# A two-block transformer on one core: sparse attention weighed in column halves, scaling shared by DVE and POOL, and waits and splits moved in three other stages

## Chip, cores and metric

The kernel runs on one core of a Trainium2 chip, as one program that is launched once. The metric is the device time of an execution in microseconds; a smaller time is better. Everything is computed in float32: PE takes a product either as f32 or as the sum of products of a high and a low part of its operands (type fp32r, names with hi and lo).

## What is computed

256 tokens of 1024 features pass through two blocks of two layers each.

```
first_block:   twice: h += 0.5 * swiglu(rmsnorm(h));  h += merged(conv, latent attention) @ w_o
                      h += 0.5 * swiglu(rmsnorm(h));  h += sigmoid(gate) * (p @ w_ple_proj);  then rmsnorm
second_block:  layer 0: h = gla_mixer(x)   (gated linear attention, chunks of 64)
               layer 1: h = nsa_mixer(x)   (sparse attention)
               each:    x = layer_norm(ALPHA * x + h);  x = layer_norm(ALPHA * x + moe_ffn(x))
nsa_mixer:     o = g0 * attention over 15 compressed blocks
                 + g1 * attention over selected blocks + g2 * attention over a window;  o @ w_out
```

With 256 tokens every block of 64 is selected and the window covers all, so the selected and the window branch are both causal attention over all keys, with keys and values of their own. There are 16 heads of 64 features in four groups that share keys and values. A head's two branches are each softmax(q k), times its gate, times v.

## The kernel before

All five engines run queues written out by hand, in program order, tied by semaphores; there is no scheduler. The weights come as a stream of units of 128 x 2048 values. For each unit SP loads halves into a ring of three raw slots (`fetch`), ACT copies them to a high part (`split_hi`, L773 and L775), DVE subtracts that for the low part (`split_lo`, L1160), and PE multiplies (`product`, L1945: high by high, high by low, low by high). A slot is free for ACT when PE has finished the unit three earlier. `units(n)` on ACT is n such splits; on DVE it is a split, and then the work on the results of a unit two earlier, which waits for PE. What else ACT and DVE have to do stands between the units, so its place in the queue sets when a unit gets ready. On PE, `take()` waits for the low part, and `settle(leave)` waits until all but `leave` of the pending banks of results have been read.

*Feed-forward* (`gate_up`, four times 11 trips of two units): a unit gives two blocks of 128 hidden features. For each block come eight products of high weights with both parts of x (512 columns, L2053) and eight of low weights with the high part (256 columns, L2056). The down projection (L2104, L2108) goes by up to sixteen and sixteen.

*Front of linear attention:* queries, keys, then values in four units, accumulated over all four in the four banks of psa, two banks per half of the tokens; then transposes and scores, the gate r, and states. ACT does logarithm and exponentials of the decay (L1041 to L1049) around DVE's scan (L1551 to L1558). DVE copies the values out, scaled, in two operations (L1573), with one signal after both.

*Front of sparse attention:* queries, compression of keys (two units) and of values (two units), keys, values. PE rotates the queries with a fixed matrix (L2533) into psd, once ACT has read the mixing gates there with a sigmoid (L1083); DVE finishes the rotation with two operations of 2048 elements (L1796, L1798), and POOL has made the product with the cosine before (L730).

*Sparse loop:* 32 items: i = t // 4 numbers a pair of heads, two items are its branches and two its sides (t % 2: the head within the pair). In trip t PE makes the scores of item t (mask L2261, L2628), turns the probabilities of item t - 2 (L2637) and weighs item t - 3 (L2654 to L2656: probabilities stationary, 64 columns of values moving). DVE takes the two row maxima (L1890, L1891) and copies every second turned item (L1897), ACT exponentiates (L1113, L1115) and copies the others (L1108). The probabilities are left unnormalised; per pair of heads DVE scales the 512 sums by gate over denominator (L1902, L1904, L1909), POOL adds the branches (L744), and PE turns the sum with two identity products onto the compressed branch (`nsa_gather`: L2665, L2669), from where ACT and DVE split it (L1121, L1887).

## Time and profile before

| | |
|---|---|
| Time, median of 3 runs | 1945.93 us (1942.67 to 1946.19) |
| The profiled execution | 1944.6 us, span of the trace 1942.8 us |
| Busy: PE, DVE, ACT, POOL | 1918.0, 1443.4, 1099.1, 36.6 us |
| Granted PE clock, mean over the span | 0.998 of 2.4 GHz |

The span is what the trace covers; the execution's time is 1.8 us longer. The profile gives each engine's busy time, the timeline of instructions with the idle time before each and what ended it, and the chain of waits that leads to the last instruction. A PE matmul's length in it includes its way through the array, so consecutive ones overlap, and the distance of their starts is what each costs. In the names, psa and psd are the two halves of PSUM, of four banks each, arena is the shared work space in SBUF, w_hi and w_lo the parts of a unit of weights, x_both and y_both both parts of an operand.

### The profile page before, as it was taken

How to read it: one execution, taken by the hardware profiler on the slowest of the kernel's cores; microseconds unless marked ns; L12 is line 12 of the kernel's file. 1: busy time of each engine (PE TensorE's matmuls, PEld its weight loads, DVE VectorE, ACT ScalarE, POOL GpSimd, SP SyncE). 2: the span in 40 equal slices, each digit the busy share in tenths (PEclk: the TensorE clock that was granted, in tenths of full speed). 3: DMA queues.
4: the chain of work that ended last, by engine and by line, in shares of the span. 5: the costliest groups of instructions: out<-in, count | busy, mean ns of one | idle time of the engine just before them, and what ended most of it. 6: DMA issues, size and time to landing. Idle time of an engine off the chain costs nothing.

```text
span 1942.8 us, 30918 instructions
## 1 busy us (share of the span) xinstructions
PE 1918.0 (99%) x12146; PEld 1714.2 (88%) x12146; DVE 1443.4 (74%) x1867; ACT 1099.1 (57%) x1453; POOL 36.6 (2%) x37
## 2 busy tenths in 40 slices
PE   9999999999999999999999999999999999999998
PEld 7888999998889888999998889888888898997887
DVE  6775777777757776686678766775799887568997
ACT  6654545565547654555556545544677663656775
POOL 0000000000000000000000000000000010001000
PEclk9999999999999999999999999999999999999999
DMA  7656555355555566555355665442799744038994
GB/s 284 194 191 194 189 196 174 125 178 189 192 194 178 190 193 194 194 191 172 118 184 191 194 192 192 144 155 66 288 359 380 293 152 152 1 109 309 368 374 161
DMA packets 89683, 388.33 MB, mean 200 GB/s; under 512 B 10096, under 2 KB 10096, under 8 KB 74832
## 3 DMA queue, kind: packets, MB, share of 16 engines
q1 hardware_dynamic: 88992, 383.87, 57.7%
q0 software_dynamic: 560, 2.60, 0.3%
q8 instruction: 96, 1.57, 0.3%
q14 instruction: 35, 0.29, 0.0%
HBM read 385.38 MB, written 1.05 MB: 199 GB/s over the span
## 4 chain that ended last, share of the span: by engine, by line
PE 92%; DVE 4%; ACT 1%; DMA 1%; DVEq 1%; issue 1%; SPq 0%; POOL 0%; ACTq 0%
PE psa L1945 38%; PE psd L2053 9%; PE psa L2053 8%; PE psd L1945 7%; PE psd L2056 4%; PE psa L2104 4%; PE psd L2104 4%; PE psa L2056 4%; PE psd L2108 2%; PE psa L2108 2%; PE psa L2628 1%; PE psa L2275 1%; DVE w_lo L1160 1%; DMA raw<-weights 1%; PE psd L2637 1%
## 5 line engine op out<-in xcount | busy, mean ns | idle before, releaser
L1160 DVE TENSOR_TENSOR w_lo<-raw,w_hi 128x1024 fp32r<-128x1024 f32 x496 | 588.4, 1228 | 194.5 <-ACT w_hi L773 191.5
L773 ACT ACTIVATE w_hi<-raw 128x1024 fp32r<-128x1024 f32 x250 | 263.4, 1054 | 296.7 <-PE psa L1945 171.2
L1945 PE MATMUL psa<-x_both,w_hi 128*128 128x256 f32 x1984 | 360.7, 284 | 1.2 <-DVE arena L1573 0.7
L1945 PEld LDWEIGHTS psa<-x_both,w_hi 128*128 128x128 f32 x1984 | 309.7, 192 | 2.8 <-DVE arena L1573 0.9
L1945 PE MATMUL psa<-x_both,w_lo 128*128 128x256 f32 x992 | 280.6, 283 | 0.0
L775 ACT ACTIVATE w_hi<-raw 128x1024 fp32r<-128x1024 f32 x250 | 261.4, 1046 | 4.9 <-DMA raw<-weights 4.9
L1945 PE MATMUL psa<-w_hi,slots_x 128*128 128x512 f32 x640 | 201.8, 396 | 0.7 <-DVE w_lo L1155 0.5
L1945 PEld LDWEIGHTS psa<-x_both,w_lo 128*128 128x128 f32 x992 | 190.3, 192 | 0.0
L1155 DVE TENSOR_TENSOR w_lo<-raw,w_hi 128x2048 fp32r<-128x2048 f32 x60 | 138.9, 2315 | 12.3 <-ACT w_hi L768 11.3
L1945 PEld LDWEIGHTS psa<-w_hi,slots_x 128*128 128x128 f32 x640 | 116.6, 188 | 25.6 <-DVE w_lo L1155 2.5
L1945 PE MATMUL psa<-w_lo,slots_x 128*128 128x512 f32 x320 | 125.2, 391 | 0.0
L768 ACT ACTIVATE w_hi<-raw 128x2048 fp32r<-128x2048 f32 x60 | 114.9, 1915 | 9.8 <-PE psd L1945 9.8
L1945 PE MATMUL psa<-y_both,w_hi 128*128 128x256 f32 x608 | 110.4, 284 | 1.8 <-issue 1.8
L2053 PE MATMUL psd<-x_both,w_hi 128*128 128x512 f32 x384 | 98.8, 394 | 0.6 <-DVE x_both L1179 0.6
L1945 PE MATMUL psd<-w_hi,x_both 128*128 128x512 f32 x320 | 99.0, 390 | 0.0
L2053 PE MATMUL psd<-y_both,w_hi 128*128 128x512 f32 x384 | 98.6, 393 | 0.0
L1945 PEld LDWEIGHTS psa<-y_both,w_hi 128*128 128x128 f32 x608 | 94.9, 192 | 2.2 <-ACT arena L1016 2.1
L1155 DVE TENSOR_TENSOR w_lo<-raw_y,w_hi 128x2048 fp32r<-128x2048 f32 x36 | 85.5, 2374 | 13.4 <-ACT w_hi L768 13.4
L2104 PE MATMUL psa<-hid_both,w_hi 128*128 128x512 f32 x352 | 86.6, 391 | 0.0
L2104 PE MATMUL psd<-hid_both,w_hi 128*128 128x512 f32 x352 | 86.6, 391 | 0.0
L1945 PE MATMUL psa<-y_both,w_lo 128*128 128x256 f32 x304 | 86.0, 283 | 0.0
L2053 PE MATMUL psa<-x_both,w_hi 128*128 128x512 f32 x320 | 80.2, 392 | 1.0 <-DVE act_gate L1193 1.0
(423 smaller groups left out, 3487.2 us busy)
## 6 DMA issues: line engine op xcount, KB each, us to landing
raw<-weights SPq DMA_DIRECT2D x500, 512.0 KB, 4.8
raw<-weights SPq DMA_DIRECT2D x60, 1024.0 KB, 6.8
raw_y<-weights SPq DMA_DIRECT2D x36, 1024.0 KB, 6.8
x<-weights SPq DMA_DIRECT2D x18, 1024.0 KB, 6.4
h<-x_in SPq DMA_DIRECT2D x1, 1024.0 KB, 5.0
result<-h SPq DMA_DIRECT2D x2, 512.0 KB, 2.8
sml<-smalls POOLq DMA_DIRECT2D x1, 831.0 KB, 10.3
cst<-consts POOLq DMA_DIRECT2D x1, 683.5 KB, 7.7
```

Of the source, the lines that this page charges most:

```text
L768: act.activation(w_hi[:, s, :], raws[r], ACT.Copy).then_inc(hi_done, 2)
L773: act.activation(w_hi[:, s, UNIT_HALVES[0]], raw[:, s, UNIT_HALVES[0]], ACT.Copy).then_inc(hi_done, 1)
L775: act.activation(w_hi[:, s, UNIT_HALVES[1]], raw[:, s, UNIT_HALVES[1]], ACT.Copy).then_inc(hi_done, 1)
L1155: dve.tensor_tensor(w_lo[:, s, :], raws[r], w_hi[:, s, :], ALU.subtract).then_inc(lo_done, 2)
L1160: dve.tensor_tensor(w_lo[:, s, c], raw[:, s, c], w_hi[:, s, c], ALU.subtract).then_inc(lo_done, 1)
L1945: ins = pe.matmul(out, lhs, rhs, start=first and n == 0, stop=last and n == 2, skip_group_check=True)
L2053: pe.matmul(out, hi, operand[2][:, :, k, :], start=k == 0, stop=False, skip_group_check=True)
L2056: ins = pe.matmul(out[:, 0:T], lo, operand[0][:, k, :], start=False, stop=k == KD - 1, skip_group_check=True)
L2104: pe.matmul(out, parts(s, at * P, at * P + P)[0], hid_both[:, k], start=k == 0, stop=False, skip_group_check=True)
L2108: ins = pe.matmul(out[:, 0:T], parts(s, at * P, at * P + P)[1], hid_both[:, k, 0, :], start=False, stop=k == HB - 1, skip_group_check=True)
L2275: ins = pe.matmul(out[:, P * tt:P * tt + keys], a, b, start=False, stop=tt == 1 and n == len(terms) - 1, skip_group_check=True)
L2628: ins = pe.matmul(out[:, P * tt:P * tt + keys], nsa_q[:, i, tt * P:tt * P + P], (nsa_ks, nsa_kw)[branch][:, i // 4, side_of, 0:keys], star ...
```

## The change

**Sparse loop.** Scores use four banks of psa rather than three, and probabilities four buffers each before and after turning. The denominators are kept per item, and DVE makes for each item, one trip after its maxima, a reciprocal, a product with the gate and the scaling of the first 128 columns; POOL scales the other 256; only then may PE turn the item (three trips after its scores). PE weighs two items, both sides, at every second trip: the values are stationary now, 64 columns each, and the two sides write partitions 0 to 63 and 64 to 127 of a bank of psd, on which the compressed branch was put first. The scaled sums, their addition by POOL and the identity products are gone. The last projection waits for the last two pieces of its operand, where it waited for one.

**Feed-forward.** A unit does the high products of both blocks and then the low ones of both; first_half is signalled behind the first block's low products.

**Front of linear attention.** PE waits for the last bank before the values only where it writes that bank; DVE signals the values of the first half of the tokens on their own, and PE goes on when their two banks are free. ACT splits one unit more before the three exponentials, one less behind.

**Front of sparse attention.** ACT's sigmoid comes one unit earlier. On DVE the first hidden-row copy and two units' splits come before the two 2048-wide operations of the rotation.

```diff
@@ gpsimd
-            for i in range(KD):
-                pool.wait_ge(parts_ready, i + 1)
...
+            for t in range(2 * NHEADS):
+                pool.wait_ge(share_ready, t + 1)
+                part = nsa_probs[:, t % 4, P:384]
+                pool.tensor_scalar(part, part, nsa_share[:, t % 4, 1:2], None, ALU.mult).then_inc(p_ready, 1)
@@ scalar, linear attention
             act.activation(gla_t, gla_t, ACT.Ln, bias=1.0).then_inc(act_out, 1)
-            units(1)
+            units(2)
...
             act.activation(gla_kend, gla_t, ACT.Exp, scale=1.0 / GTAU).then_inc(act_out, 1)
-            units(4)
+            units(3)
@@ scalar, sparse front
-            units(3)
+            units(2)
             act.wait_ge(pe_to_act, seen.more(pe_to_act))
             act.activation(nsa_gates, psd[:, 0, 0:96].rearrange("p (a c) -> p a c", a=2),
                            ACT.Sigmoid).then_inc(mix_known, 1)
-            units(1 + 2 + 1)
+            units(1 + 1 + 2 + 1)
@@ scalar, sparse loop
-            for t in range(items + 7):
-                if 0 <= t - 2 < items:
+            for t in range(items + 5):
+                if 0 <= t - 3 < items:
...
-                if t >= 10 and (t - 10) % 4 == 0:
-                    i = (t - 10) // 4
+                if t >= 8 and t % 4 == 0:
+                    i = (t - 8) // 4
                     act.wait_ge(o_summed, seen.more(o_summed))
-                    act.activation(y_hi[:, i, :], psa[:, 3, 0:T], ACT.Copy).then_inc(xh_ready, 1)
+                    act.activation(y_hi[:, i, :], psd[:, 2 + i % 2, 0:T], ACT.Copy).then_inc(xh_ready, 1)
@@ vector, linear attention, values_scaled
                                             psa[:, 2 * tt:2 * tt + 2, :], rms_by_token[:, tt:tt + 1], None, ALU.mult)
+                    if tt == 0:
+                        ins.then_inc(evac, 1)
@@ vector, sparse front
             mark(for_pe)
             units(1, None)
+
+            def hidden_rows(kind, bank):
+                return lambda _: dve.tensor_copy(nsa_hid_rows[0:CROWS, kind, :], psa[0:CROWS, bank, 0:CHID])
+            units(1, hidden_rows(0, 3))
+            units(1, None)
             dve.wait_ge(pe_out, seen.more(pe_out))
             dve.wait_ge(queries_by_cos, 1)
...
-            units(1, hidden_rows(0, 3))
-            units(1, None)
@@ vector, sparse loop
+                if 0 <= t - 1 < items:
+                    u = t - 1
+                    i, branch, side_of = u // 4, u % 4 // 2, u % 2
+                    dve.wait_ge(exp_done, seen.more(exp_done))
+                    step(dve.reciprocal(nsa_share[:, u % 4], nsa_den[:, u % 4]))
+                    step(dve.tensor_tensor(nsa_share[:, u % 4], nsa_share[:, u % 4], g_c[:, :, 2 * i + side_of, 1 + branch],
+                                           ALU.mult))
+                    part = nsa_probs[:, u % 4, 0:P]
+                    dve.tensor_scalar(part, part, nsa_share[:, u % 4, 0:1], None, ALU.mult).then_inc(share_ready, 1)
+                if 0 <= t - 3 < items:
                     turn_of_t = seen.more(t_done)
-                    if t % 2 == 1:
+                    if (t - 3) % 2 == 1:
                         dve.wait_ge(t_done, turn_of_t)
-                        dve.tensor_copy(nsa_probs_t[1], psd[:, 1, 0:384]).then_inc(odd_pt_ready, 1)
...
+                        dve.tensor_copy(nsa_probs_t[:, (t - 3) % 4], psd[:, 1, 0:384]).then_inc(odd_pt_ready, 1)
@@ tensor, gate_up
-                    else:
-                        ins = block(0, range(KD))
-                        if part == 1:
-                            ins.then_inc(first_half, 1)
-                        ins = block(1, range(KD))
+                        for j in range(2):
+                            high(j, ks)
+                        for j in range(2):
+                            ins = low(j, ks)
+                            if part == 1 and j == 0:
+                                ins.then_inc(first_half, 1)
@@ tensor, linear attention
-            settle()
+            settle(1)
             for m in range(4):
...
                         for half in range(2):
+                            if tt == 1 and half == 1:
+
+                                settle()
...
-            pending.append(evac)
+            pending += [evac, evac]
...
-            settle()
+            settle(1)
...
+            settle(2)
             dense(2, KD, 2, x, signal=r_scaled, bank=2)
@@ tensor, sparse loop
             def nsa_weigh(t):
...
+                i, branch = t // 4, t % 4 // 2
+                out = psd[:, 2 + i % 2, 0:T]
+                if branch == 0:
...
+                    pe.matmul(out, nsa_vc[:, i // 4, i % 2, :], nsa_pt[:, i // 2, :], start=True, stop=False,
+                              skip_group_check=True)
+                pe.wait_ge(odd_pt_ready, seen.more(odd_pt_ready))
+                for k in range(TT):
+                    for side_of in range(2):
+                        keys = nsa_probs_t[:, (t + side_of) % 4, (0, T)[k]:(T, 384)[k]]
+                        ins = pe.matmul(out[DH * side_of:DH * side_of + DH, P * k:T],
+                                        nsa_v[:, branch, k, 2 * (i // 4) + side_of, :], keys, start=False,
+                                        stop=branch == 1 and k == 1, skip_group_check=True)
...
+            for t in range(items + 4):
                 if t < items:
                     nsa_score(t)
-                if 0 <= t - 2 < items:
-                    nsa_turn(t - 2)
+                if t >= 5 and t % 2 == 1:
+
+                    pe.wait_ge(pt_ready, seen.more(pt_ready))
                 if 0 <= t - 3 < items:
-                    nsa_weigh(t - 3)
+                    nsa_turn(t - 3)
...
+                if t >= 5 and t % 2 == 1:
+                    nsa_weigh(t - 5)
-            out_projection((KD - 1,), o_done, late_residual=True)
+            out_projection((KD - 2, KD - 1), o_done, late_residual=True)
```

Three places show how the instructions stand. On PE in the middle of the sparse loop, one item before:

```order
L2261 MATMUL psa<-mask_bf,ident_bf 128x2x128
L2628 MATMUL psa<-arena 128x128
L2628 MATMUL psa<-arena 128x256
L2637 MATMUL psd<-cst,arena 128x128 [waits exp_done]
L2637 MATMUL psd<-cst,arena 128x128 x2
L2654 MATMUL psd<-arena 128x64 [waits odd_pt_ready]
L2655 MATMUL psd<-arena 128x64
L2656 MATMUL psd<-arena 128x64
```

and in the change, the second trip of a pair:

```order
L2250 MATMUL psa<-mask_bf,ident_bf 128x2x128
L2621 MATMUL psa<-arena 128x128
L2621 MATMUL psa<-arena 128x256
L2630 MATMUL psd<-cst,arena 128x128 [waits p_ready,pt_ready]
L2630 MATMUL psd<-cst,arena 128x128 x2
L2643 MATMUL psd<-arena 128x256 [waits o_done]
L2649 MATMUL psd<-arena 64x256 [waits odd_pt_ready]
L2649 MATMUL psd<-arena 64x256
L2649 MATMUL psd<-arena 64x128 x2
```

The turns now wait for POOL's p_ready in place of ACT's exp_done, the trip before has no weighing, and the compressed product (L2643, every second time) stands here and not in a gather of its own.

On DVE in the sparse loop, a trip with a copy, before and in the change:

```order
L1890 TENSOR_REDUCE arena<-psa 128x1 [waits s_done]
L1891 TENSOR_REDUCE arena<-psa 128x1
L1897 COPY arena<-psd 128x384 [waits t_done]
```

```order
L1886 TENSOR_REDUCE arena<-psa 128x1 [waits s_done]
L1887 TENSOR_REDUCE arena<-psa 128x1
L1893 RECIPROCAL arena<-arena 128x2 [waits exp_done]
L1894 TENSOR_TENSOR arena<-arena 128x2 [waits dve_step]
L1897 TENSOR_SCALAR arena<-arena 128x128 [waits dve_step]
L1902 COPY arena<-psd 128x384 [waits t_done]
```

The copy, for which PE's weighing waits, stands three operations further from the scores.

On DVE in the front of sparse attention, before and in the change (the operations of 2048 elements are the rotation, those of 62x256 the hidden rows):

```order
L1160 TENSOR_TENSOR w_lo<-raw,w_hi 128x1024 [waits hi_done] x2
L1796 TENSOR_TENSOR arena<-psd,cst 128x2048 [waits queries_by_cos,pe_out]
L1798 TENSOR_TENSOR arena<-arena,x 128x2048 [waits dve_step]
L1160 TENSOR_TENSOR w_lo<-raw,w_hi 128x1024 [waits dve_step,hi_done]
L1160 TENSOR_TENSOR w_lo<-raw,w_hi 128x1024 [waits hi_done]
L1802 COPY arena<-psa 62x256 [waits unit_done]
L1160 TENSOR_TENSOR w_lo<-raw,w_hi 128x1024 [waits hi_done] x2
L1806 TENSOR_SCALAR arena<-arena 128x96 [waits mix_known]
```

```order
L1154 TENSOR_TENSOR w_lo<-raw,w_hi 128x1024 [waits hi_done] x4
L1792 COPY arena<-psa 62x256 [waits unit_done]
L1154 TENSOR_TENSOR w_lo<-raw,w_hi 128x1024 [waits hi_done] x2
L1797 TENSOR_TENSOR arena<-psd,cst 128x2048 [waits queries_by_cos,pe_out]
L1799 TENSOR_TENSOR arena<-arena,x 128x2048 [waits dve_step]
L1802 TENSOR_SCALAR arena<-arena 128x96 [waits dve_step,mix_known]
```

Two units are subtracted (four halves) in one go, and the rotation stands behind the first hidden rows and a third unit.

## Rows read from the trace of the kernel before

**Rows 1.** The page, part 1: busy us, share of span, instructions by engine
```profile
PE 1918.0 (99%) x12146; PEld 1714.2 (88%) x12146; DVE 1443.4 (74%) x1867; ACT 1099.1 (57%) x1453; POOL 36.6 (2%) x37
```

**Rows 2.** Timeline, PE, feed-forward: start us, length us, engine, line, operation, tiles
```profile
60.64 2.00 PE L2053 MATMUL psd<-x_both,w_hi 128*128 128x512 f32 x8
...
66.22 2.00 PE L2053 MATMUL psd<-x_both,w_hi 128*128 128x512 f32 x8
...
138.85 3.82 PE L2104 MATMUL psa<-hid_both,w_hi 128*128 128x512 f32 x16
...
144.42 1.55 PE L2104 MATMUL psa<-hid_both,w_hi 128*128 128x512 f32 x6
```

**Rows 3.** Timeline, PE, front of linear attention; [idle us before <-releaser]
```profile
1257.15 0.71 PE L1945 MATMUL psa<-w_hi,x_both 128*128 128x512 f32 x2 [0.99 <-DVE arena L1193]
...
1270.27 0.74 PE L1945 MATMUL psa<-w_hi,x_both 128*128 128x512 f32 x2 [1.97 <-DVE w_lo L1160]
...
1284.83 0.50 PE L1945 MATMUL psa<-x_both,w_hi 128*128 128x256 f32 x2 [0.68 <-DVE arena L1573]
...
1291.27 2.86 PE L2461 MATMUL psd<-arena 128*128 128x256 f32 x12 [0.44 <-DVEq L1141]
```

**Rows 4.** Timeline, ACT and DVE, the same front
```profile
1263.92 1.06 ACT L1047 ACTIVATE arena<-arena 128x1024 f32<-128x1024 f32 x1 [6.66 <-DVE arena L1558]
...
1267.85 2.36 DVE L1160 TENSOR_TENSOR w_lo<-raw,w_hi 128x1024 fp32r<-128x1024 f32 x2 [3.97 <-ACT w_hi L773]
...
1270.37 2.36 DVE L1160 TENSOR_TENSOR w_lo<-raw,w_hi 128x1024 fp32r<-128x1024 f32 x2 [0.16 <-issue]
```

**Rows 5.** Timeline, all engines, front of sparse attention
```profile
1592.25 1.04 ACT L775 ACTIVATE w_hi<-raw 128x1024 fp32r<-128x1024 f32 x1
...
1597.80 4.57 POOL L730 TENSOR_TENSOR x<-arena,cst 128x2048 f32<-128x2048 f32 x1 [29.94 <-DVEq L1141]
...
1598.13 6.45 DVE L1160 TENSOR_TENSOR w_lo<-raw,w_hi 128x1024 fp32r<-128x1024 f32 x2 [0.46 <-ACT w_hi L773]
...
1599.07 1.28 ACT L1083 ACT_TABLE_LOAD   x1
...
1600.76 3.67 PE L2533 MATMUL psd<-arena,cst 128*128 128x512 f32 x8 [1.00 <-ACT arena L1083]
...
1609.25 2.36 DVE L1160 TENSOR_TENSOR w_lo<-raw,w_hi 128x1024 fp32r<-128x1024 f32 x2
...
1611.67 0.45 PE L1945 MATMUL psa<-w_hi,y_both 128*62 128x256 f32 x2 [1.59 <-DVE w_lo L1160]
```

**Rows 6.** Timeline, PE, from full tiles to 62-column ones
```profile
1596.66 0.28 PE L1945 MATMUL psa<-x_both,w_lo 128*128 128x256 f32 x1
1596.78 0.40 PE L1945 MATMUL psa<-w_hi,y_both 128*62 128x256 f32 x2
```

**Rows 7.** The chain that ended last, sparse loop: start, length (us), what
```profile
1664.41 0.66 PE psa L2628 x4
...
1672.19 0.66 PE psa L2628 x4
```

**Rows 8.** Timeline, PE and DVE, one item of the sparse loop
```profile
1654.66 0.27 PE L2261 MATMUL psa<-mask_bf,ident_bf 128*128 128x256 bf16 x1
...
1655.42 0.49 PE L2637 MATMUL psd<-cst,arena 128*128 128x128 f32 x3
...
1655.62 0.29 DVE L1890 TENSOR_REDUCE arena<-psa 128x1 f32<-128x128 f32 x1 [1.09 <-PE psa L2628]
...
1656.16 0.55 DVE L1897 COPY arena<-psd 128x384 f32<-128x384 f32 x1
```

**Rows 9.** Timeline, DVE, latent attention of the first block
```profile
336.26 0.15 DVE L1330 RECIPROCAL stats<-stats 128x2 f32<-128x2 f32 x1
...
336.65 0.35 DVE L1333 TENSOR_SCALAR arena<-arena,stats 128x256 f32<-128x256 f32 x1
```

**Rows 10.** Timeline, POOL, its sum in the sparse loop
```profile
1661.01 0.73 POOL L744 TENSOR_TENSOR arena<-arena 128x256 f32<-128x256 f32 x1 [17.74 <-DVE arena L1909]
```

More of the change, by code:

```diff
@@ L509, in two_blocks @@
         nsa_pt = view(11264, NG, T)
-        nsa_probs = view(12288, 3, 384)
-        nsa_probs_t = [view(13440 + 384 * i, 384) for i in range(2)]
+        nsa_probs = view(7168, 4, 384)
+        nsa_probs_t = view(12288, 4, 384)
         nsa_hid = view(15360, 4, 60)
@@ L1880, in _ @@
             items = 2 * NHEADS
-            seen.more(pv_done, DEPTH * NH)
             seen.more(t_done, DEPTH * NH)
-            for t in range(items + 8):
-                if t >= 11 and (t - 11) % 4 == 0:
-                    i = (t - 11) // 4
+            for t in range(items + 6):
+                if t >= 9 and t % 4 == 1:
+                    i = (t - 9) // 4
                     dve.wait_ge(xh_ready, seen.more(xh_ready))
-                    dve.tensor_tensor(y_lo[:, i, :], psa[:, 3, 0:T], y_hi[:, i, :], ALU.subtract).then_inc(o_done, 1)
+                    dve.tensor_tensor(y_lo[:, i, :], psd[:, 2 + i % 2, 0:T], y_hi[:, i, :],
+                                      ALU.subtract).then_inc(o_done, 1)
@@ L1894, in _ @@
+                if 0 <= t - 3 < items:
                     turn_of_t = seen.more(t_done)
-                    if t % 2 == 1:
+                    if (t - 3) % 2 == 1:
                         dve.wait_ge(t_done, turn_of_t)
-                        dve.tensor_copy(nsa_probs_t[1], psd[:, 1, 0:384]).then_inc(odd_pt_ready, 1)
-                if t >= 6 and (t - 6) % 4 == 0 and t - 6 < items:
-                    i = (t - 6) // 4
-                    share = nsa_share[:, i % 2]
-                    dve.wait_ge(exp_done, seen.more(exp_done, 4))
-                    step(dve.reciprocal(share, nsa_den[:, i % 2]))
-                    by_part = share.rearrange("p (a s b) -> p a s b", a=TT, s=2)
-                    dve.tensor_tensor(by_part, by_part, g_c[:, :, 2 * i:2 * i + 2, 1:3], ALU.mult)
@@ L2643, in nsa_weigh @@
-                if t == 0:
-                    pe.wait_ge(pt_copied, 1)
-                copied = (pt_ready, odd_pt_ready)[t % 2]
-                pe.wait_ge(copied, seen.more(copied))
-                if t % 4 == 0 and i >= 2:
-                    pe.wait_ge(parts_ready, seen.more(parts_ready))
-                turned_p = nsa_probs_t[t % 2]
-                v0, v1 = (nsa_v[:, branch, k, 2 * (i // 4) + side_of, :] for k in range(TT))
-                c = P * side_of + DH * branch
-                low, high = psd[:, 2 + i % 2, c:c + DH], psd[:, 2 + i % 2, T + c:T + c + DH]
@@ L2673, in _ @@
+                if branch == 1:
+                    ins.then_inc(o_summed, 1)
             items = 2 * NHEADS
[L2674 to L2675 removed]
+            for t in range(items + 4):
                 if t < items:
                     nsa_score(t)
[L2678 to L2679 removed]
+                if t >= 5 and t % 2 == 1:
+                    pe.wait_ge(pt_ready, seen.more(pt_ready))
                 if 0 <= t - 3 < items:
[L2681 removed]
+                    nsa_turn(t - 3)
```

89 lines of the change are left out of this document (25 added, 64 removed).

## Prediction

> **What bounds the kernel now.** I read the page first: PE is busy for 99% of the span and DVE for 74% [rows 1], and the chain of work that ended last is PE almost throughout. So an edit counts only as far as it shortens PE's own work or removes one of PE's waits, and each term below is read from the timeline of the stage that the edit touches. There are four such places. In the feed-forward stage PE never waits; one unit of weights for gate or up is two blocks of eight high and eight low products, and takes 5.58 us from 60.64 to 66.22 [rows 2]. In the front of linear attention PE waits four times: 0.99, 1.97, 0.68 and 0.44 us [rows 3], together 4.08. In the front of sparse attention it waits twice, 1.00 us for the sigmoid and 1.59 us for a low half of weights [rows 5]. In the sparse loop it doesn't wait in steady state: four items and one gather take 7.78 us, from 1664.41 to 1672.19 [rows 7], so a pair of items takes 3.89.
>
> The profiled execution took 1944.6 us, 1.3 below the median of the runs (1945.9). The sum is made against 1944.6, and 1.3 is added at its end.
>
> **Feed-forward: eight and eight become sixteen and sixteen.** Nothing is added or removed; a unit switches between high and low products twice fewer. The down projection already runs sixteen and sixteen of the same shapes: 138.85 to 144.42, 5.57 us [rows 2]. Against 5.58 that is 0.01, with rounding up to 0.02; I take 0.015 for the 84 units outside the four that come in pieces (4 feed-forwards x 11 trips x 2, less 4): **-1.3 us**, ends 0 and -3. The signal first_half comes one block of high products later, but still 0.95 before the unit's end, where ACT now arrives because of its splits. I cost that at nothing; the cover is ACT's splitting.
>
> **Linear attention.** The split of the high half of value unit 2 moves ahead of ACT's three exponentials. ACT stands idle 6.66 us there, until DVE's scan chain ends [rows 4]; the split (2 us) fits, its slot is free since PE waits at 1257.15, and its weights were asked for a ring of three earlier. DVE can then subtract unit 2 right behind that chain, at 1263.9, rather than at 1267.85. Unit 3's high half now follows the exponentials, so unit 3 is subtracted at 1267.85 where it was 1270.37 [rows 4]: everything that DVE does behind it is 2.52 earlier. PE's waits of 0.99 (only bank 3 is held now), 1.97 and 0.68 go, 3.64 in all, but the fourth, before the state products at 1291.27 [rows 3], is for that same DVE chain and moves by 2.52 only: it grows from 0.44 to 1.56. What is late next is thus DVE's copies and masks. **-2.5 us**; ends -1.0 (only the first wait goes) and -4.1 (all four).
>
> **Sparse front.** The sigmoid with its table load (1.28) ran behind the split that ends just before 1599.07; now it runs behind the one that ends at 1593.29 [rows 5], so it is done before 1595, and PE starts the rotation at 1599.76: -1.00. On DVE the split of the second value-compression unit moves ahead of the two 2048-wide rope operations: from 1609.25 to right behind the pair that ends at 1604.58 [rows 5]. It is ready at 1607, PE wants it at 1609.1, and the wait of 1.59 goes too. The rope operations (4.67 us between those two rows) now stand in front of the second hidden-row copy, on which PE's transposes wait; I count that copy ready at 1617.8, just as PE arrives (2.59 earlier than now), and the key copy behind it about 0.3 late. **-2.3 us**; ends -1.0 and -2.6.
>
> **Sparse loop.** PE loses the two identity products per group and DVE the 512-wide scaling; weighing costs, per pair of items, two matmuls of 256 columns and two of 128, which write the two halves of the partitions. The scores of one item take 384 columns in 0.66 us [rows 7], so 768 columns are 1.32 one after another. If the halves overlap, in program order (each f32 matmul is two passes, and a half's passes can't overlap each other), the second pass of each runs beside the first of its partner: two thirds, 0.88. If they overlap fully, 0.66. No row shows two halves; I take 0.88 as the middle, and keep both ends.
>
> But PE's work no longer sets the pace. 3.89 less half of a group's identity products (0.2) and a third of the weighing (0.44) is some 3.3. What ends last is a loop through DVE. PE may weigh a pair only when DVE has copied the odd item's turned probabilities, and DVE does this behind that iteration's maxima, reciprocal, gate product and scaling. From the end of PE's scores to DVE's first maximum are 0.20 us (1655.42 to 1655.62) and from it to the next operation 0.54 [rows 8]; reciprocal and first scaling are 0.39 (336.26 to 336.65) [rows 9] and the new gate product is another 0.20, like the reciprocal; the copy is 0.55 [rows 8]. With 0.10 for PE's restart (between 0 and 0.20, the hand-over the other way) that is 1.98 after the scores; then the weighing, 0.88, and the next item's scores with their mask, 0.77 (1654.66 to 1655.42 is 0.76): **3.63 us a pair** for 3.89. POOL's scaling of 256 columns is bounded by its 0.73 for two inputs [rows 10] and nothing below; it has over an iteration until PE turns the item, so I cost it at nothing; it would bind only from about 1.7 us. The first and the last items wait for one whole chain, as now, and I count 15 pairs: 15 x 0.26 = **-3.9 us**; ends -7.2 (full overlap) and +2.7 (none).
>
> The sum is -1.3 - 2.5 - 2.3 - 3.9 = -10.0: 1934.6 against the profiled execution, **1935.9 us** against the median. Nothing downstream gives it back: PE has no wait over 0.7 us behind the loop.
>
> **A rule against this change.** Where PE goes from full tiles to narrower ones, the next matmul starts after the usual 0.12 us (1596.66 to 1596.78) [rows 6]; so I add nothing for the 32 such changes in the loop. The Trainium skill (TensorEngine Tiling (Array Packing), Key Properties) says that changing the tiling mode drains TensorE, and also that different tiles can load and multiply in parallel. The trace contradicts the first for that case, unless the 62-column tile counts as no change; the second no run here shows. What a drain would cost here, by rows: PE's hand-over, 0.20 us, twice a pair, 15 x 0.40 = 6.0 us.
>
> **The rivals.**
> (a) *The halves run one after another.* Then a pair takes 3.63 + 0.44 = 4.07, longer than now, and the loop costs +2.7 rather than -3.9: 1942.5 us, no change that can be told. For it: nothing in this trace shows an overlap; against it only that the halves use different parts of the array. With drains as well, 1948.5.
> (b) *They overlap fully, or PE's restart is free:* 3.41 a pair, 1932.6 us.
> (c) *POOL and DVE exclude each other (slower).* In the front one subtraction on DVE that reads two operands from SBUF stretches: two halves take 6.45 us from 1598.13 where a pair elsewhere takes 2.36 [rows 4, 5], while POOL multiplies for 4.57 [rows 5]. In the loop POOL now works in every item. If DVE's operations meet it each time, 0.73 per item is added to the loop, 30 x 0.73 = 21.9: 1957.8 us. It decides as soon as POOL's scaling lasts beyond DVE's two maxima, 0.54 [rows 8], and these are held too. Against it: the maxima read PSUM, and in the loop of now they run beside POOL's sum and take no longer than elsewhere. The Trainium skill (SBUF — State Buffer, who interferes with whom) has the two engines share one port pair that is held for a whole instruction, and tensor_reduce free of it; by that rule only the reciprocal to scaling could meet POOL, and these come after the maxima.
> (d) *The edits of the fronts give nothing* (the waits come back one step later): -5.2 left, 1940.7 us.
>
> **How the numbers follow.** My own sum has 0.50, (a) 0.20 (a quarter of it with drains), (b) 0.15, (c) 0.05, (d) 0.10. A measurement of this kernel tells about 0.2% from no change, 3.9 us here: faster is below 1942.0, slower above 1949.8. The sum, (b), and (d) lie below, (a) lies on the border with most of it inside no change; this gives 0.77 faster, 0.17 the same and 0.06 slower. The range goes from (b) with the feed-forward term at its far end, 1930.5, to (a) with some of a front lost, 1944.
>
> **What would show it.** In the profile after: units of gate and up at 5.57 us; PE's waits near 1257, 1270 and 1285 gone and one of some 1.6 before the state products; no wait before the rotation or the last compression unit; in the loop a period of 3.6 per pair, PE idle 0.5 before every second or each weighing with DVE's copy named as releaser, the two halves' matmuls starting less than a full pass apart, and POOL's scaling under 0.73. I am wrong if the period is set by PE without gaps (halves serial), if POOL is the releaser of PE's turns, or if DVE's reciprocal starts late behind POOL.

## The result, and the profile after

| | before | the change |
|---|---|---|
| Median of 6 runs each | 1946.06 us (1942.67 to 1948.13) | 1931.53 us (1931.01 to 1933.57) |
| Ratio to before | | 0.9928, 95% interval 0.9915 to 0.9940 |
| Profiled execution, its span | 1944.6, 1942.8 us | 1933.57, 1931.4 us |

The kernel got faster by 14.5 us, where 10.0 was forecast. The profiled execution of the change is the slowest of its six, and it is 11.0 below that of before. The sections on the experiments and on the forecast show why these two differences differ. Two executions behind the medians further down, 2798.93 us of ffn_only and 6042.99 us of sparse_loop_only, were slow ones: the ratios leave them out, and without them these medians would be 1943.77 and 1940.64.

The page, part 1, against [rows 1]: PE lost 10.4 us of busy time and 103 matmul records (a few records can be missing from a trace), DVE gained 9.7 us and POOL 24.

```profile
PE 1907.6 (99%) x12043; PEld 1696.9 (88%) x12050; DVE 1453.1 (75%) x1939; ACT 1103.4 (57%) x1453; POOL 60.8 (3%) x61
```

**Feed-forward**, timeline of PE, as [rows 2]. A unit is now one row of sixteen and one of sixteen, from 59.84 to 65.41: 5.57 us for 5.58.

```profile
59.84 3.82 PE L2041 MATMUL psd<-x_both,w_hi 128*128 128x512 f32 x16
63.50 2.08 PE L2046 MATMUL psd<-x_both,w_lo 128*128 128x256 f32 x16
65.41 0.86 PE L2041 MATMUL psd<-x_both,w_hi 128*128 128x512 f32 x3
```

**Front of linear attention**, timelines of PE and DVE, as [rows 3, 4]. The waits of 0.99 and 1.97 are gone. That of 0.68 is still 0.58, and the fourth grew from 0.44 to 1.60.

```profile
1253.72 0.63 PE L1935 MATMUL psa<-w_hi,x_both 128*128 128x512 f32 x2
...
1278.92 0.50 PE L1935 MATMUL psa<-x_both,w_hi 128*128 128x256 f32 x2 [0.58 <-DVE arena L1567]
...
1286.53 0.70 PE L2453 MATMUL psd<-arena 128*128 128x256 f32 x2 [1.60 <-DVEq L1135]
```

```profile
1265.65 2.36 DVE L1154 TENSOR_TENSOR w_lo<-raw,w_hi 128x1024 fp32r<-128x1024 f32 x2 [1.77 <-ACT w_hi L770]
1268.17 1.23 DVE L1557 TENSOR_TENSOR arena<-arena 128x1024 f32<-128x1024 f32 x1 [0.16 <-issue]
1269.43 1.22 DVE L1558 TENSOR_TENSOR arena<-arena 128x1024 f32<-128x1024 f32 x1
1270.58 1.22 DVE L1559 SCALAR_TENSOR_TENSOR arena<-arena 128x1024 f32<-128x1024 f32 x1
1272.37 1.76 DVE L1561 MEMSET arena<- 128x2048 f32 x1 [0.58 <-issue]
1274.30 0.91 DVE L1562 MEMSET arena<- 128x1024 f32 x1 [0.16 <-issue]
1275.13 2.29 DVE L1154 TENSOR_TENSOR w_lo<-raw,w_hi 128x1024 fp32r<-128x1024 f32 x2
1277.58 2.48 DVE L1567 TENSOR_SCALAR arena<-psa,stats 128x1024 f32<-128x1024 f32 x2 [0.16 <-issue]
```

From 1265.65 on DVE waits for no other engine; its idle times of 0.16 and 0.58 are put down to issue. Its copy of the values starts at 1277.58 and PE waits for the first half of it: DVE is what is late in this stage now.

**Front of sparse attention**, timeline, as [rows 5]. The sigmoid runs early, the rotation starts at 1595.06 with no wait, and the last compression unit has none either. What is new is 0.25 before the hidden rows' turns, and a short wait behind the keys: in the kernel before the products of 128x60 follow those of 128x64 without a gap (1628.81), in the change they start 0.12 behind their end.

```profile
1588.78 1.28 ACT L1080 ACT_TABLE_LOAD   x1
...
1593.27 4.58 POOL L728 TENSOR_TENSOR x<-arena,cst 128x2048 f32<-128x2048 f32 x1 [29.95 <-DVEq L1135]
...
1593.60 8.73 DVE L1154 TENSOR_TENSOR w_lo<-raw,w_hi 128x1024 fp32r<-128x1024 f32 x4 [0.46 <-ACT w_hi L770]
...
1613.12 0.43 PE L2560 MATMUL psd<-cst,arena 62*128 62x62 f32 x4 [0.25 <-DVE arena L1792]
...
1619.72 1.95 PE L2574 MATMUL psd<-sml,arena 128*128 128x64 f32 x16
1621.79 0.43 PE L2579 MATMUL psd<-arena,cst 128*128 128x60 f32 x2
```

**Sparse loop**, timeline of one pair with PE, DVE and POOL, as [rows 7, 8, 10].

```profile
1666.41 0.49 PE L2630 MATMUL psd<-cst,arena 128*128 128x128 f32 x3
1666.61 0.29 DVE L1886 TENSOR_REDUCE arena<-psa 128x1 f32<-128x128 f32 x1 [0.72 <-PE psa L2621]
...
1667.15 0.15 DVE L1893 RECIPROCAL arena<-arena 128x2 f32<-128x2 f32 x1
...
1667.54 0.29 DVE L1897 TENSOR_SCALAR arena<-arena 128x128 f32<-128x128 f32 x1
...
1667.74 0.55 DVE L1902 COPY arena<-psd 128x384 f32<-128x384 f32 x1
1667.83 0.60 PE L2643 MATMUL psd<-arena 128*128 128x256 f32 x2
1667.92 0.92 POOL L742 TENSOR_SCALAR arena<-arena 128x256 f32<-128x256 f32 x1 [1.01 <-DVE arena L1897]
...
1668.36 0.87 PE L2649 MATMUL psd<-arena 128*64 128x256 f32 x8
...
1669.16 0.28 PE L2250 MATMUL psa<-mask_bf,ident_bf 128*128 128x256 bf16 x1
```

The forecast's chain can be read off it. Scores end where the turn starts (1666.41), and then come 0.20 to the maxima, 0.54 to the reciprocal, 0.59 to the copy, 0.55 for the copy, 0.07 to the weighing (1668.36), 0.80 to the next mask (1669.16) and 0.78 for its scores: 3.53 us. The masks of pairs are 3.52 apart on average (1662.12 to 1669.16 is two). The eight passes of a weighing (two matmuls of 256 columns and two of 128, each in two passes) take 0.87 from the first start to the last end.

In this pair, which has the compressed product (L2643), PE has no gap either: its own work and the chain through DVE end together. In the other pair, which has none, PE waits for DVE's copy, as forecast, though for 0.16 and not 0.5 us. The turn before that starts late as well. The second turn of such a pair starts 0.15 us behind the end of POOL's scaling, 0.82 after the first score where 0.66 is usual; the wait for DVE's copy that follows hides this.

```profile
1663.08 0.92 POOL L742 TENSOR_SCALAR arena<-arena 128x256 f32<-128x256 f32 x1 [1.29 <-DVE arena L1897]
...
1663.33 0.82 PE L2621 MATMUL psa<-arena 128*128 128x128 f32 x4
...
1664.15 0.52 PE L2630 MATMUL psd<-cst,arena 128*128 128x128 f32 x3
1664.22 0.55 DVE L1902 COPY arena<-psd 128x384 f32<-128x384 f32 x1
...
1664.83 0.87 PE L2649 MATMUL psd<-arena 128*64 128x256 f32 x8 [0.16 <-DVE arena L1902]
```

At both ends of the loop POOL is the releaser that PE waits for: before the first turn, as below, and for 0.88 us before a turn at 1695.24.

```profile
1644.02 0.55 PE L2630 MATMUL psd<-cst,arena 128*128 128x128 f32 x3 [1.11 <-POOL arena L742]
```

### The profile page after: what moved, and what is told of

The parts are those of the page before. It is cut to its first block, busy times and chain, and to the rows that moved or that the text cites. A ratio compares the mean times of both kernels' runs of the same rounds, so it can differ in the third digit from the quotient of the medians.

```text
span 1931.4 us, 30816 instructions
## 1 busy us (share of the span) xinstructions
PE 1907.6 (99%) x12043; PEld 1696.9 (88%) x12050; DVE 1453.1 (75%) x1939; ACT 1103.4 (57%) x1453; POOL 60.8 (3%) x61
## 3 DMA queue, kind: packets, MB, share of 16 engines
q8 instruction: 95, 1.56, 0.3%
## 4 chain that ended last, share of the span: by engine, by line
PE 91%; DVE 5%; ACT 1%; DMA 1%; DVEq 1%; issue 1%; SPq 0%; POOL 0%; ACTq 0%
PE psa L1935 38%; PE psd L2041 9%; PE psa L2041 8%; PE psd L1935 7%; PE psd L2046 4%; PE psa L2093 4%; PE psd L2093 4%; PE psa L2046 4%; PE psd L2097 2%; PE psa L2097 2%; DVE w_lo L1154 1%; PE psa L2264 1%; DMA raw<-weights 1%; PE psa L2621 1%; PE psd L2649 1%
## 5 line engine op out<-in xcount | busy, mean ns | idle before, releaser
L2041 PE MATMUL psd<-x_both,w_hi 128*128 128x512 f32 x384 | 93.3, 392 | 1.5 <-DVE w_lo L1154 0.9
L2041 PE MATMUL psd<-y_both,w_hi 128*128 128x512 f32 x384 | 93.1, 392 | 0.0
L2041 PEld LDWEIGHTS psd<-x_both,w_hi 128*128 128x128 f32 x384 | 70.3, 188 | 15.6 <-DVE w_lo L1154 1.4
## 6 DMA issues: line engine op xcount, KB each, us to landing
sml<-smalls POOLq DMA_DIRECT2D x1, 831.0 KB, 10.4
```

The lines of the kernel that those rows point to most:

```text
L2041: pe.matmul(acc[:, 2 * part + j, :], parts(s, (2 * k + j) * P, (2 * k + j + 1) * P)[0], operand[2][:, :, k, :], start=k == 0, stop=False, ...
```

## The experiments

Stages are compared by the distance of the same two PE instructions in two traces. Where nothing in a stage was changed, these repeat to 0.02 us: the loop, from its first scores to the first product of the projection, took 64.76 or 64.77 us in each of the five traces that have it as before. The medians of whole kernels move by a microsecond or two from one comparison to the next; the kernel before had 1946.06, 1944.50, 1944.48, 1945.21 and 1943.85.

### One part at a time

Each of four kernels is the kernel before with one part of the diff shown above, and nothing else.

```diff
# ffn_only: @@ tensor, gate_up
# linear_only: @@ scalar, vector and tensor, linear attention
# sparse_front_only: @@ scalar and vector, sparse front
# sparse_loop_only: @@ gpsimd, and scalar, vector and tensor, sparse loop
```

> The kernel before with the feed-forward part alone. Theory 1 (the four parts add up, each is seen in its own stage): units of gate and up at 5.57 us for 5.585, 84 times, is -1.4, and the first two trips, whose high and low products come in pieces, gain the 0.7 that the trace after shows up to its start of the second block of units; -2.1 to -2.3 in all, 1943.8 for 1946.1. Theory 2 (the parts help each other: splits that come earlier in one stage feed the next): under -1.5 here.

> The kernel before with the linear-attention part alone. Theory 1: the three waits of 0.99, 1.97 and about 0.1 of 0.68 us go, the wait before the state products grows from 0.44 to 1.6, so PE reaches the state products 2.0 to 2.5 earlier: -2.3. Theory 2: what is gained is waited for again at the next fixed point (the wait of 0.87 before the last outputs, 1.57 before the output projection) and the run is within 1 us of before.

> The kernel before with the sparse front alone. Theory 1: the waits of 1.00 and 1.59 us go and 0.25 comes back before the fixed-matrix products behind the keys: -2.3 to -2.9. Theory 2 (POOL's product of 4.57 us stretches DVE's subtraction whatever stands in front): no more than -1.0, the sigmoid's wait alone.

> The kernel before with the sparse loop alone. Theory 1: the period of a pair is 3.52 us as in the trace after, from first scores to the last projection 59.8 us for 64.9, -5.0. Theory 2: part of these 5 us came from the earlier front (weights of the last projection split earlier): -3.5 to -4.0. By my forecast (3.63 a pair) it would be -3.9.

| kernel | median, us (before 1944.50) | ratio (95%) | its stage, by the traces |
|---|---|---|---|
| ffn_only | 1943.92 | 0.9995 (0.9986 to 1.0004) | -0.40 in each of the last three feed-forwards |
| linear_only | 1942.07 | 0.9989 (0.9980 to 0.9998) | 41.41 to 38.95, -2.46 |
| sparse_front_only | 1941.93 | 0.9985 (0.9977 to 0.9994) | -2.47 |
| sparse_loop_only | 1940.78 | 0.9979 (0.9971 to 0.9988) | 64.76 to 59.71, -5.05 |

(Linear attention: from the last matmul of the decay's gate to the first state product. Sparse front: from the last layer norm's small products to the products with a fixed matrix behind the keys.)

The stage lengths of the whole change are the same: 38.95, -2.46 and 59.72. So the stage lengths add up and none feeds another, as theory 1 says of each part. The medians are less exact: they fall by 0.6, 2.4, 2.6 and 3.7 us, 9.3 in all. The feed-forward's total, though, is not the 2.1 to 2.3 that I expected, but four times 0.40. The rest that I expected lies ahead of 27 us, and there the traces vary. At the first unit of the second trip, at 27.01 in the trace of before, the kernels with the feed-forward part are 0.30 to 1.02 earlier than that trace and those without it 0.36 to 0.85, so no gain can be told there. The whole change's stages give -1.6 - 2.46 - 2.47 - 5.04 = -11.6 us.

A gain of 0.40 for the 22 units of a feed-forward is 0.018 each, and the traces say where it comes from. In the trips between 40 and 130 us of before, the starts of a block's high products are 0.2333, 0.2359, 0.2283, 0.2325 and 0.2309 us apart at first and 0.2267 from the sixth distance on; of low products the first pair is 0.1133 apart and the others 0.12. In the change they are the same by position, and all of the ninth to sixteenth are at 0.2267. So a change from low to high costs 0.027 and gives back 0.008, and the edit saves one of two: 0.020.

### The clock

> The changed kernel once more, unaltered. The sparse loop from first scores to the last projection takes 59.7 us again, to 0.05, since stages repeat to 0.02 in the four runs before; the time is 1931 to 1934 and what differs from the first profile lies in the stretches where the granted clock is 0.5, worth 1 to 2.5 us each.

The kernel took 1932.42 us (1931.18 to 1933.27), ratio 0.9932 (0.9919 to 0.9946), its loop 59.71 and its linear stage 38.95. Against the 1944.48 of this comparison that is 12.1 us less, not 14.5. What differs between executions of one kernel is where the granted clock falls to 0.50, the lower level of 1.2 GHz, for a few microseconds. In the first trace of the change this happened around 1732, in the products of 16 columns before the norm behind the loop (view of windows: length, busy time of PE, PEld, DVE, ACT and POOL, granted clock, DMA share, GB/s):

```profile
1726.00:1728.00 2.00, 1.94 (x16) 1.65 (x16) 1.47 (x3) 1.97 (x3) 0.00 (x0) 1.00 0.03 8
1730.00:1732.00 2.00, 2.00 (x17) 2.00 (x17) 1.13 (x1) 1.78 (x2) 0.00 (x0) 0.81 0.95 401
1732.00:1734.00 2.00, 2.00 (x11) 2.00 (x11) 1.93 (x6) 0.79 (x2) 0.00 (x0) 0.50 1.01 418
1734.00:1736.00 2.00, 1.93 (x10) 1.81 (x10) 1.71 (x9) 1.23 (x4) 0.00 (x0) 0.50 1.02 430
1736.00:1738.00 2.00, 1.85 (x5) 0.75 (x5) 1.37 (x3) 1.85 (x2) 0.00 (x0) 0.50 1.00 418
1738.00:1740.00 2.00, 2.00 (x15) 1.39 (x14) 0.33 (x2) 0.00 (x0) 0.00 (x0) 0.98 0.86 365
```

PE began these products 13.5 us earlier than before (1744.93 there) and was 11.35 earlier behind the norm (from 1752.03 on). In the trace of before the clock was full there, and fell at 1365 and 1635 instead, where the lead of the change grows by 0.6 and 1.6 us that no edit explains; near 1330, where it fell in the change alone, the lead shrinks by 0.7. In the other traces the places are, with one exception that is told below, among five, near 1330, 1365, 1635, 1740 and 1940, each in a stretch of short matmuls or waits, and an execution has between one and four of them. The runs of one kernel spread over 1 to 6 us. The lowest times of the first comparison, 1942.67 and 1931.01, differ by 11.7 us, and the stages say 11.6. The rest of the 14.5 would then be such stretches. In the 74 later executions of the kernel before the time goes with the mean granted clock of the execution: the medians are 1943.2 us at 0.998, 1944.4 at 0.997, 1946.9 at 0.996 and 1948.5 at 0.995. The median of the first comparison, 1946.06, lies above all later ones, 1943.85 to 1945.21. But the clock of its six runs was not recorded one by one, so for these six it remains argued.

### What the two column halves do

```diff
# same_columns
-pe.matmul(out[DH * side_of:DH * side_of + DH, P * k:T],
+pe.matmul(out[0:DH, P * k:T],
# side_after_side
-for k in range(TT):
-    for side_of in range(2):
+for side_of in range(2):
+    for k in range(TT):
```

> The changed kernel with both sides' weighing in the first 64 columns of the array (the second side's sums are added to the first's, so the upper half of the attention output is left out); the same instructions and sizes. Theory 1 (the halves overlap fully): their passes follow one another, 1.32 us for 0.66 a pair, on the loop that sets the pace: period 4.18, +9.9 us, the loop 69.6. Theory 2 (a matmul of 64 columns is cheap by itself): within 1 us of the change.

> The changed kernel with the two matmuls of one side before the two of the other, same positions. Theory 1 (matmuls start in program order, and one that waits for its own half holds those behind it): only the end of the first side overlaps the start of the second, some 1.15 us for 0.66: period 4.0, +7 us, the loop 67. Theory 2 (each half has a queue of its own): no change. Theory 3 (nothing overlaps when the neighbours use one half): 1.32 us, +9.9.

Measured: same_columns 1942.20 us (ratio 0.9984, 0.9975 to 0.9994), loop 69.37; side_after_side 1932.82 (0.9934, 0.9919 to 0.9950), loop 59.81. The timelines of PE, the weighing and the next mask, of the first and of the second:

```profile
1667.34 1.51 PE L2649 MATMUL psd<-arena 128*64 128x256 f32 x8 [0.35 <-DVE arena L1902]
1668.79 0.28 PE L2250 MATMUL psa<-mask_bf,ident_bf 128*128 128x256 bf16 x1
```

```profile
1666.26 0.88 PE L2649 MATMUL psd<-arena 128*64 128x256 f32 x8 [0.17 <-DVE arena L1902]
1667.07 0.28 PE L2250 MATMUL psa<-mask_bf,ident_bf 128*128 128x256 bf16 x1
```

In one half the eight passes take 1.45 us to the next mask for 0.80, and the loop 9.65 more (forecast 9.9): a matmul into one half is no cheaper by itself, and in the change the two halves' passes run beside each other. (This kernel leaves out the upper half of the attention output.) The second kernel was a surprise. With both matmuls of a side next to each other nothing is lost (0.10 us in the whole loop), so PE does not hold the second side's matmuls behind the first side's: theory 2 holds, each half takes its own in order. My forecast of 0.88 for a weighing rested on program order and falls with this.

The Trainium skill (TensorEngine Tiling (Array Packing), Key Properties) has both: different tiles multiply in parallel, with which same_columns agrees, and a change of tiling mode drains the engine. Whether it drains no row shows, but such a change has a small price here. From the last pass of a weighing to the mask the starts are 0.205 us apart, where 0.109 is usual for that length, and behind a compressed product the weighing starts 0.53 after it instead of 0.43: 0.2 us a pair, half of the 0.40 at which I priced a drain. The row with 62 columns, on which I had put the price at nothing, does not carry over to these matmuls.

### What sets the pace of the loop

```diff
# copy_first: DVE, in each trip
 dve.tensor_reduce(... ALU.max, negate=True).then_inc(nmax_ready, 1)
+if 0 <= t - 3 < items:  # the copy of the odd turned item
+    ...
 if 0 <= t - 1 < items:  # reciprocal, product, scaling
     ...
-if 0 <= t - 3 < items:
-    ...
# dve_scales_all
-pool.tensor_scalar(part, part, nsa_share[:, t % 4, 1:2], None, ALU.mult).then_inc(p_ready, 1)
+part = nsa_probs[:, u % 4, P:384]
+dve.tensor_scalar(part, part, nsa_share[:, u % 4, 1:2], None, ALU.mult).then_inc(p_ready, 1)
```

> The changed kernel with DVE's copy of the odd item ahead of reciprocal, product and scaling. Theory 1 (the pace is the loop through DVE: 0.20 + 0.54 + 0.59 + 0.55 + 0.07 + weighing 0.80 + scores 0.78 = 3.53): the 0.59 leaves the loop and PE's own work sets the pace, twice 0.78 for mask and scores, twice 0.33 for a turn, 0.80 for weighing and half of 0.44 for the compressed product, 3.23 a pair: 15 x 0.29 = -4.4 us, the loop 55.3. Theory 2 (POOL's 0.92 us of scaling is the bound, since PE's turn already waits for it by 0.16): the scaling comes 0.55 later and the period stays at 3.5 or grows to 3.9.

> The changed kernel with POOL's scaling of 256 columns done by DVE, behind its 128. Theory 1 (POOL's work is hidden and costs DVE nothing): the loop through DVE grows by one operation of 256 elements, 0.35 to 0.42 us: period 3.9, the loop 65 for 59.7. Theory 2 (POOL's scaling holds DVE up, my rival (c)): the other operations of DVE get shorter by what they now lose, and the loop grows by less than 3 us.

copy_first: 1929.71 us (ratio 0.9921, 0.9907 to 0.9934), loop 58.14 for 59.72. It gained 1.6, not 4.4. Theory 2 in its strong form falls, since the period shrank: pairs now take 3.53 and 3.28 in turn, where they took 3.53 and 3.52. Theory 1 named the right loop but the wrong floor. A pair with a compressed product takes 3.53 on PE by itself, 0.77 and 0.33 twice, 0.53 and 0.81: I had averaged it with the other pair, left out the change of tile, and taken the distance of starts too small. The other pair takes 3.28, because its turn waits 0.16 for POOL's scaling (PE starts 0.15 behind POOL's end at 1669.43):

```profile
1668.51 0.92 POOL L742 TENSOR_SCALAR arena<-arena 128x256 f32<-128x256 f32 x1 [0.82 <-DVE arena L1902]
...
1669.58 0.52 PE L2630 MATMUL psd<-cst,arena 128*128 128x128 f32 x3
```

dve_scales_all: 1937.05 us (0.9957, 0.9942 to 0.9973), loop 63.49, a pair 3.78. Its 3.8 us lie between the two expectations, and the trace decides. Without POOL in the loop DVE's reciprocal, product and scaling take 155, 161 and 287 ns on average. In the change the first two take 155 and 162 where POOL is idle and 157 and 162 where it works beside them, and the scaling 287; in copy_first, where POOL works beside some of the scalings, these take 287 too. POOL costs DVE nothing here, and rival (c) is out. What I mis-sized is the step: two DVE operations in a row overlap at their ends, so one of 256 elements that lasts 0.35 moves the next by 0.26 (1659.66 to 1659.92), and 15 x 0.26 = 3.9.

```profile
1659.45 0.29 DVE L1893 TENSOR_SCALAR arena<-arena 128x128 f32<-128x128 f32 x1
1659.66 0.34 DVE L1895 TENSOR_SCALAR arena<-arena 128x256 f32<-128x256 f32 x1
1659.92 0.55 DVE L1900 COPY arena<-psd 128x384 f32<-128x384 f32 x1
```

### The waits per bank alone, and a faster version

linear_waits_only is linear_only with ACT's splits where they were before. low_last_zeros_on_pool builds on copy_first.

```diff
# linear_waits_only, on linear_only
-units(2)
+units(1)
 ... the three exponentials ...
-units(3)
+units(4)
# low_last_zeros_on_pool, on copy_first: the low half's subtraction at the end of a trip of DVE, and
+pool.wait_ge(scanned, 1)
+pool.memset(gla_kt, 0.0)
+pool.memset(gla_scores, 0.0).then_inc(zeroed, 1)
@@ vector
+mark(scanned)
-dve.memset(gla_kt, 0.0)
-dve.memset(gla_scores, 0.0)
...
+dve.wait_ge(zeroed, 1)
```

> The kernel before with the waits per bank of linear attention alone; ACT splits as before. Theory 1 (each wait has its own cause): the wait of 0.99 before the values goes, 1.1 with its restart, the one of 1.97 grows to 3.0, since its split still stands behind the exponentials at the end of a chain that doesn't start at PE: within 0.3 us of before at the state products. Theory 2 (the scan chain moves with PE): 1.1 stay.

> The copy ahead of the reciprocal, and two more moves. In the loop DVE's subtraction for a group's low half comes after the copy and the scaling rather than before the maxima; in linear attention the two clearings of 2.67 us are made by POOL behind DVE's scan. Theory 1 (in the loop with the copy first the pair without compressed product takes 3.28 because PE's turn waits 0.16 for POOL, whose scaling stands behind the subtraction; in linear attention DVE is what is late): the loop takes 56.9 to 57.2 for 58.1, and from the first value product to the state products PE takes 30.3 to 30.8 us for 32.8, since its waits of 0.58 and 1.60 go. Theory 2 (POOL and DVE exclude each other here as POOL's product of 4.57 us does in the sparse front, where one subtraction takes 5.32 for 1.21): DVE loses there what it saves, and the value stage takes 32 us or more.

> The kernel of low_last_zeros_on_pool once more, unaltered, because its stages are 2.7 us shorter than those of copy_first while its median was 0.6 higher. Theory 1 (the difference is stretches at a granted clock of 0.50, each about 3.4 us long and worth up to 1.7, of which its first profile had four and that of copy_first almost none): the loop takes 57.2 and from the first value product to the state products 31.0 again, and the median lies at 1927.5 to 1930. Theory 2 (POOL's clearings or the new order cost something outside these stages): the median stays above 1930 and a stage outside is longer at full clock.

linear_waits_only: 1944.88 us for 1945.21 (0.9996, 0.9987 to 1.0005), no difference. The wait of 0.99 goes and the next one grows from 1.97 to 3.19; the stage from the gate to the state products is 41.95, even longer than before (41.41). So the waits per bank, taken alone, only move a wait, and with ACT's order added the stage gains 2.46. ACT's order without the waits per bank was not run. The 0.54 on top comes from the clock: towards the end of the long wait it fell to 0.50, a place where no other trace has it. PE, which was 0.41 ahead of the trace of before at 1269.86, was 0.81 behind it at 1272.58, and DVE's copy of the values, which never waits for PE in the trace of before, waited 0.70 for it. Windows, then DVE's row:

```profile
1268.00:1270.00 2.00, 0.14 (x1) 0.14 (x1) 1.84 (x3) 2.00 (x3) 0.00 (x0) 0.84 0.08 12
1270.00:1272.00 2.00, 2.00 (x5) 1.61 (x6) 2.00 (x2) 2.00 (x3) 0.00 (x0) 0.50 0.77 254
1272.00:1274.00 2.00, 2.00 (x8) 1.59 (x8) 1.80 (x3) 0.14 (x1) 0.00 (x0) 0.81 0.86 262
```

```profile
1282.42 2.48 DVE L1573 TENSOR_SCALAR arena<-psa,stats 128x1024 f32<-128x1024 f32 x2 [0.70 <-PE psa L1947]
```

low_last_zeros_on_pool: 1930.28 us (0.9915, 0.9902 to 0.9929), its loop 57.22 (expected 56.9 to 57.2) and from the first value product to the state products 31.04 (32.81 in the change, 30.3 to 30.8 expected: it stayed short of theory 1 by a quarter of a microsecond, the 0.67 that PE still waits). PE's wait of 0.58 is gone and that of 1.60 is down to 0.67. POOL's clearings do not hold DVE up (timelines of the second run of this kernel):

```profile
1260.18 1.81 POOL L719 MEMSET arena<- 128x2048 f32 x1 [1234.93 <-DVEq L1140]
1261.93 0.95 POOL L720 MEMSET arena<- 128x1024 f32 x1
```

```profile
1260.21 1.22 DVE L1558 TENSOR_TENSOR arena<-arena 128x1024 f32<-128x1024 f32 x1
1261.36 2.35 DVE L1159 TENSOR_TENSOR w_lo<-raw,w_hi 128x1024 fp32r<-128x1024 f32 x2
```

Its median was above that of copy_first although its stages are 0.92 and 1.77 shorter. Run again it took 1929.00 us (1926.02 to 1930.48, ratio 0.9924, 0.9910 to 0.9937), the same stages to 0.03 (57.19 and 31.04). The two traces with hardly any low clock are those of copy_first and of this second run, 1929.05 and 1926.02 us: 3.0 apart, where the stages say 2.7 and the start 0.2. Theory 1 holds, up to the medians, which still have 1929.1 over the ten runs of both comparisons beside 1929.7. The stages show it as the fastest version here; against the change it is 4.3 us shorter in them (2.5 in the loop, 1.8 in linear attention).

## Why the forecast came out as it did

The time lies in the range and on the forecast side; 14.5 us came where 10.0 was said. It lies nearer to rival (b)'s 1932.6 than to my 1935.9, but that is not to (b)'s credit: its period of 3.41 a pair was not reached. Point by point:

- **Feed-forward, -1.3 forecast, -1.6 measured.** Right in kind and near in size. Unit times read to 0.01 gave 0.015 each; the distances of starts give 0.020. Delaying first_half cost nothing.
- **Linear attention, -2.5 forecast, -2.46 measured, by luck: two errors cancel.** "PE's waits of 0.99, 1.97 and 0.68 go, 3.64 in all" was wrong for the third, which stayed at 0.58. The fourth grew to 1.60, as forecast (1.56). The other error is the price of a wait. In the trace of before the matmul behind the idle 1.97 starts 2.36 after its predecessor, where 0.23 is usual, and its successor starts 0.11 late: 2.25 for a wait of 1.97. Idle time is counted from the end of the last matmul, which the next one would have overlapped. The forecast counted idle time alone.
- **Sparse front, -2.3 forecast, -2.47 measured.** Both waits went, worth 1.2 and 1.8 for their 1.00 and 1.59 by the same rule. The hidden rows' copy, which I had put at "ready just as PE arrives", is late and costs 0.3 (0.25 of idle time and the restart). The key copy "about 0.3 late" came as forecast: PE's lead over the kernel before falls from 7.30 to 6.97 us at the products of 60 columns behind it.
- **Sparse loop, -3.9 forecast, -5.04 measured.** The mechanism was right for every second pair, where DVE's copy is the releaser of PE's weighing; in the others PE's own 3.53 ends with it, and "some 3.3" for PE's own work is right only as the mean of the two kinds (3.53, and 3.10 in the last kernel, where neither DVE nor POOL holds the second kind up). Right too were five of the seven terms of the pace to 0.01 (0.20, 0.54, 0.59, 0.55, 0.77). The mis-sized ones are the weighing, 0.80 for 0.88, and PE's restart, 0.07 for 0.10: 3.52 for 3.63. Rival (b) had the halves right (they overlap fully) and lacked the 0.14 around them, mostly the change of tile. 15 x 0.37 is 5.5; the ends of the loop take back 0.5, chiefly by the wait of 1.11 for POOL before the first turn (0.13 before).
- **POOL.** "Bounded by its 0.73 for two inputs" was wrong: one input and a scale per row take 0.92. Costing it at nothing held for the pace alone. One of my signs of being wrong, POOL as the releaser of PE's turns, did appear: before the first turn (1.11), at the end (0.88) and, hidden by a later wait, in every second pair. "The first and the last items wait for one whole chain, as now" overlooked that this chain is now longer by DVE's three operations and POOL's scaling. "Over an iteration until PE turns the item" left out that DVE starts an item's scaling late.
- **Changes of tile.** They were put at nothing and cost 0.2 us a pair. Of that, 0.10 lies behind the weighing and so on the chain through DVE.
- **The sum.** The stages give -11.6, so 1.6 us of the miss are terms, 1.1 of them the loop. The other 2.9 of the medians' difference is no part of the change as far as the traces can tell; I took the median of three runs as the kernel's time and the profile of one execution as typical.
- **The rivals.** (a) is refuted by same_columns, (c) by dve_scales_all, (d) by the fronts' stages. In the sparse front POOL and DVE do exclude each other, one subtraction took 5.33 us there beside POOL's product; in the loop and beside POOL's clearings no operation got longer.

## What to carry to other kernels

When PE is the bound, price a wait by the distance of the starts around it, not by the idle time that the profile prints, and price an inserted DVE operation by the distance to its successor, not by its length; both corrections were 0.1 to 0.3 us each here. In a software pipeline write down the loop through the engines that sets the pace, and look at what stands in the queue ahead of the one operation that the bound engine waits for: moving DVE's copy ahead of three operations that nobody needed yet gave 1.6 us for no work. And compare stages between traces rather than medians where the effect is less than the spread of the clock.

## What was not expected of the hardware

- Matmuls for the two column halves overlap even when the program gives two for one half and then two for the other: 0.88 us for all eight passes, for 1.51 in one half.
- The first six products of 512 columns behind a block of 256-column ones start 0.228 to 0.236 us apart, later ones 0.2267.
- POOL's multiplication of 128x256 by a scalar per row took 0.92 us, more than its addition of two such tiles (0.73 in [rows 10]).
- Beside POOL's product of 128x2048 one DVE subtraction of two SBUF operands took 5.33 us for 1.21, yet POOL's clearing of 128x2048 left DVE's operations of the same kind at 1.22 and its scaling left DVE's product of 128x2 at 0.16.
- During a wait of 3.19 us without a matmul the granted clock fell to 0.50, in the one trace with such a wait; with the wait of 1.97 us at the same place it stayed full in every trace.
